# First mixer in three single-pass matmuls per product, its input weights laid out by use, and the expert biases handled ahead of the spatial gating

## The reference, cut to what matters

```
proj = x @ w_in + b_in                      # 1024 -> 512 q, 128 k, 128 v, 512 u, 512 g
attn = sliding_window_attention(q, k, v, sinks)      # 8 query heads, 2 kv heads, window 128
u = gelu(u);  g = layer_norm per group (gelu(g))     # 8 groups of 64
mixed = einsum('gts,bcsgd->bctgd', tril(w_spatial), g) + b_spatial
mix = concat([attn, u * mixed]) @ w_out + b_out
h = layer_norm(alpha * x + mix)
ffn = routed_experts(h, ...)                # 32 experts, top 4, each 1024 -> 2 x 1024 -> 1024
```

## Time and profile before

| what | value |
|---|---|
| median of 3 runs | 1468.22 us (1468.15 to 1469.3) |
| the profiled execution, its own time | 1469.2 us |
| its span | 1467.4 us |
| TensorE busy | 1396.6 us, 95% |
| VectorE, ScalarE, GpSimd busy | 535.3, 341.7, 90.1 us |
| bytes read from HBM | 489.54 MB, 334 GB/s over the span |
| first expert matmul on ring weights | 112.70 us |

### The profile page before, as it was taken

How to read it: one execution, slowest core, us unless ns; L and a number is a source line. 1 busy time by engine, 2 the same in 40 slices (tenths; PEclk the granted TensorE clock), 3 DMA queues, 4 the chain that set the end, 5 groups by cost and what they waited for, 6 DMA issues and landing times.

```text
span 1467.4 us, 23484 instructions
## 1 busy us (share of the span) xinstructions
PE 1396.6 (95%) x10106; PEld 787.6 (54%) x10106; DVE 535.3 (36%) x980; ACT 341.7 (23%) x504; POOL 90.1 (6%) x44
## 2 busy tenths in 40 slices
PE   7999999999999999999998998999999999999998
PEld 6553333333333333333333333333979999899997
DVE  1772111211211111121111111213989658777766
ACT  0531001100100010010000000102765543444442
POOL 0000000000000000000000000002000050122232
PEclk9999999999999999999999999999999999999999
DMA  9699999999999999999999999999544214255552
GB/s 362 261 403 416 428 429 427 428 433 431 430 426 436 430 430 426 435 430 431 429 427 434 427 431 434 430 427 384 182 146 142 77 42 160 91 197 186 191 181 86
DMA packets 37060, 491.36 MB, mean 335 GB/s; under 512 B 4112, under 2 KB 4624, under 8 KB 12592
## 3 DMA queue, kind: packets, MB, share of 16 engines
q1 hardware_dynamic: 36864, 490.47, 80.9%
q10 hardware_dynamic: 144, 0.13, 0.0%
HBM read 489.54 MB, written 1.05 MB: 334 GB/s over the span
## 4 chain that ended last, share of the span: by engine, by line
PE 72%; DMA 24%; DVE 2%; ACT 1%; issue 1%; SPq 0%; DVEq 0%; ACTq 0%
PE bank L905 20%; DMA ring<-in_w_exp 15%; PE bank L934 10%; DMA work<-in_w_exp 8%; PE bank L962 8%; PE bank L963 8%; PE bank L964 8%; PE bank L856 3%; PE bank L844 2%; PE bank L715 2%; PE bank L767 2%; PE bank L685 1%; ACT spare L1551 1%; PE bank L864 1%; PE bank L925 1%; PE bank L920 1%
## 5 line engine op out<-in xcount | busy, mean ns | idle before, releaser
L905 PE MATMUL bank<-ring,spare 128*64 128x512 f32 x1344 | 303.4, 604 | 20.5 <-DMA ring<-in_w_exp 20.3
L2080 DVE TENSOR_SCALAR work<-bank 128x512 f32<-128x512 f32 x32 | 22.1, 692 | 736.6 <-PE bank L905 736.6
L905 PEld LDWEIGHTS bank<-ring,spare 128*64 128x64 f32 x1344 | 97.5, 139 | 214.0 <-issue 183.1
L934 PE MATMUL bank<-ring,spare 128*64 128x512 f32 x672 | 148.8, 595 | 14.7 <-ACT spare L1551 14.7
L963 PE MATMUL bank<-work_parts,ring_parts 128*128 128x256 f32 x568 | 159.3, 281 | 0.0
L1547 ACT ACTIVATE work<-work 128x512 f32<-128x512 f32 x32 | 20.2, 631 | 530.8 <-DVE work L2080 530.8
L905 PE MATMUL bank<-work,spare 128*64 128x512 f32 x576 | 129.6, 600 | 5.3 <-DMA work<-in_w_exp 5.3
L963 PEld LDWEIGHTS bank<-work_parts,ring_parts 128*128 128x128 f32 x568 | 107.7, 190 | 1.1
L934 PEld LDWEIGHTS bank<-ring,spare 128*64 128x64 f32 x672 | 46.9, 137 | 103.1 <-issue 87.4
L962 PE MATMUL bank<-hn_hi,ring_parts 128*128 128x256 f32 x352 | 99.3, 282 | 0.0
L964 PE MATMUL bank<-hn_hi,ring_parts 128*128 128x256 f32 x352 | 99.0, 281 | 0.0
(11 more groups left out here) (467 smaller groups left out, 1980.6 us busy)
## 6 DMA issues: line engine op xcount, KB each, us to landing
ring<-in_w_exp SPq DMA_DIRECT2D x42, 4096.0 KB, 31.6
ring<-in_w_exp SPq DMA_DIRECT2D x42, 2048.0 KB, 26.2
work<-in_w_exp SPq DMA_DIRECT2D x14, 4096.0 KB, 33.0
work<-in_w_exp SPq DMA_DIRECT2D x26, 2048.0 KB, 28.7
spare<-in_w_exp SPq DMA_DIRECT2D x12, 2048.0 KB, 27.8
ring<-in_ffn_up SPq DMA_DIRECT2D x22, 1024.0 KB, 4.8
ring<-in_ffn_down SPq DMA_DIRECT2D x22, 512.0 KB, 3.4
ring<-in_w_in SPq DMA_DIRECT2D x2, 2048.0 KB, 17.2
```

What stands on the lines that cost most here:

```text
L905: ins = pe.matmul(to[n2 * CAP:(n2 + 1) * CAP, :], x_e[:, 4 * j + 2 * half + kk, :], w[:, b, kk, n2 * BANK:(n2 + 1) * BANK], start=False, s ...
L934: ins = pe.matmul(y_bank[n2 * CAP:(n2 + 1) * CAP, :], hidT[:, k % 4, k // 4 * CAP:(k // 4 + 1) * CAP], w[:, kk, n2 * BANK:(n2 + 1) * BANK] ...
```

## The change

- q/k (k = 1 to 7), g and u are computed in three fp32r passes. v, and q/k for k = 0, stay in float32. ScalarE casts x, the q/k columns, g and u to their upper parts (`in_hi`); VectorE subtracts these to get the rests (`in_lo`), in place of the raw weights. TensorE waits for these counts for each k of q/k, and for each half of g and u.
- The input weights are three tensors (w_qkv, w_g, w_u), each contiguous in its columns. The first loads come in five pieces (k = 0, 1, 2 to 3, 4 to 5, 6 to 7). w_g comes ahead of the constants, w_u behind the rows.
- v goes to bank 6; its part for k = 4 to 7 comes behind all of q/k. The scores of tile 0 no longer wait for v.
- u of tile 0 comes ahead of the transposes of the probabilities, u of tile 1 in two halves among and behind them, ahead of the attention matmuls. The spatial mixing stands between the two token tiles of the first half of `project_out`, which starts on each pair of k as its attention copy is ready.
- On SyncE, half of area 0 is issued at proj_done 2, half of area 4 and the other half of area 0 at proj_done 4, x at proj_done 6, and at attn_done 2 the expert biases, the layer norm rows and area 1.
- On VectorE, the first bias subtraction comes ahead of the gating, the second behind it, ahead of the copies of the turned u; the scaling of x comes behind these copies. The mask of wsT goes to GpSimd. Several semaphores are merged and their counts adapted.

```diff
-        w_in = ring[:, 0:KD * 1792].rearrange("p (k n) -> p k n", k=KD)
+        by_k = lambda a, at, n: a[:, at:at + KD * n].rearrange("p (k n) -> p k n", k=KD)
+        w_qkv, w_g, w_u = by_k(ring, 0, W_QKV), by_k(ring, G_AT, G1), by_k(ring, U_AT, G1)
...
-        first_pieces = [slice(0, 1), slice(1, 2), slice(2, 4), slice(4, KD)]
+        first_pieces = [slice(0, 1), slice(1, 2), slice(2, 4), slice(4, 6), slice(6, KD)]
...
@@ sync
-            first_half(APART, 0)
-            sp.wait_ge(attn_done, 1)
-            sp.dma_start(bias_all[0:BIAS_ROWS, :], A["bias"]).then_inc(bias_in, 16)
-            sp.wait_ge(proj_done, 6)
-            for half in range(2):
-                first_half(0, half)
+            sp.wait_ge(proj_done, 2)
+            first_half(0, 0)
+            sp.wait_ge(proj_done, 4)
+            first_half(APART, 0)
+            first_half(0, 1)
+            sp.wait_ge(proj_done, 6)
+            sp.dma_start(x_nat, A["x"].rearrange("(t p) d -> p t d", p=P)).then_inc(ln_rows_in, 16)
+            sp.wait_ge(attn_done, 2)
+            sp.dma_start(bias_all[0:BIAS_ROWS, :], A["bias"]).then_inc(bias_in, 16)
+            sp.dma_start(rows_sb[:, 0:ln2_at], A["rows"][0:ln2_at].partition_broadcast(P)).then_inc(ln_rows_in, 16)
             for half in range(2):
                 first_half(1, half)
-            sp.wait_ge(mixed_done, 1)
+            sp.wait_ge(sgu_done, 1)
             sp.wait_ge(ug_biased, 4)
             first_half(3, 0)
-            sp.wait_ge(mix_first, 1)
+            sp.wait_ge(mix_done, 1)
             first_half(2, 0)
-            sp.wait_ge(mix_done, 4)
+            sp.wait_ge(mix_done, 5)
             first_half(2, 1)
@@ tensor
+            pe.wait_ge(w_in_in[0], 32)
+            for i in range(5):
+                pe.matmul(qk_tile(i), w_qkv[:, 0, qk_cols[i]], xT[:, 0, :], start=i % 2 == 0, stop=False, skip_group_check=True)
+            project_v(0)
+            for piece in range(1, len(first_pieces)):
+                for k in range(first_pieces[piece].start, first_pieces[piece].stop):
+                    pe.wait_ge(in_hi, 2 * piece)
+                    for i in range(5):
+                        pe.matmul(qk_tile(i), qk_hi[:, k, qk_cols[i]], x_hi[:, k, :], start=False, stop=False, skip_group_check=True)
+                    pe.wait_ge(in_lo, 2 * piece - 1)
+                    for i in range(5):
+                        pe.matmul(qk_tile(i), qk_hi[:, k, qk_cols[i]], x_lo[:, k, :], start=False, stop=False, skip_group_check=True)
+                    pe.wait_ge(in_lo, 2 * piece)
+                    for i in range(5):
+                        ins = pe.matmul(qk_tile(i), qk_lo[:, k, qk_cols[i]], x_hi[:, k, :], start=False, stop=k == KD - 1, skip_group_check=True)
+                    if k < KD // 2:
+                        project_v(k)
+            ins.then_inc(proj_done, 1)
+            for k in range(KD // 2, KD):
+                ins = project_v(k)
             ins.then_inc(proj_done, 1)
...
+            def project_half(t, to, hi, lo, before, half):
+                pe.wait_ge(in_lo, IN_PARTS + before + half + 1)
+                for k in range(k_half[half].start, k_half[half].stop):
+                    ins = three_passes(bank[to][:, :], [a[:, k, t * P:(t + 1) * P] for a in (x_hi, x_lo)], (hi[:, k, :], lo[:, k, :]),
+                                       k == 0, k == KD - 1)
+                if half == 1:
                     ins.then_inc(proj_done, 1)
...
+            for half in range(2):
+                project_g(0, half)
+            pe.wait_ge(kv_ready, 3)
+            for half in range(2):
+                project_g(1, half)
+            pe.wait_ge(neg_max, 1)
+            for half in range(2):
+                project_u(0, half)
...
-            ins.then_inc(attn_done, 1)
-            project_half(1, 1, W_QKV)
...
@@ scalar
+            for i, ks in enumerate(first_pieces):
+                if i > 0:
+                    act.wait_ge(w_in_in[i], 32)
+                    act.copy(x_hi[:, ks, :], xT[:, ks, :]).then_inc(in_hi, 1)
+                    act.copy(qk_hi[:, ks, :], w_qkv[:, ks, 0:W_QK]).then_inc(in_hi, 1)
...
@@ vector
+            for half, ks in enumerate(k_half):
+                dve.wait_ge(in_hi, IN_PARTS + 2 + half + 1)
+                less(u_lo[:, ks, :], w_u[:, ks, :], u_hi[:, ks, :]).then_inc(in_lo, 1)
+
             for t, pr in enumerate((prob1, prob0)):
...
+            less_bias(1)
+            dve.wait_ge(sgu_done, 1)
             dve.wait_ge(ug_gelu, 3)
             for b in range(2):
...
             dve.tensor_tensor(u_nat, u_nat, sq, ALU.mult).then_inc(sgu_ready, 1)
-            for n in range(1, SPLITS):
-                dve.wait_ge(bias_cast, n)
...
+            less_bias(2)
             for b in range(2):
-                dve.wait_ge(sguT_done, b + 1)
+                dve.wait_ge(sgu_done, b + 2)
                 dve.tensor_copy(mixT[:, 4 + 2 * b:6 + 2 * b, :], bank[(2, 7)[b]][:, :].rearrange("p (k t) -> p k t", k=2)).then_inc(sguT_ready, 1)
```

More of the change, by code:

```diff
@@ L677, in _, with three_passes @@
         def _(pe):
[L679 to L688, removed]
-                for t in range(TT):
-                    ins = pe.matmul(bank[2][:, T + t * P:T + (t + 1) * P], xT[:, k, t * P:(t + 1) * P], w_in[:, k, W_QK:W_QKV],
-                                    start=False, stop=last, skip_group_check=True)
+            def three_passes(to, left, right, start, stop):
+                pe.matmul(to, left[0], right[0], start=start, stop=False, skip_group_check=True)
+                pe.matmul(to, left[0], right[1], start=False, stop=False, skip_group_check=True)
+                return pe.matmul(to, left[1], right[0], start=False, stop=stop, skip_group_check=True)
@@ new lines, in _, with project_v @@
+            qk_tile = lambda i: bank[i // 2][:, (i % 2) * T:(i % 2 + 1) * T]
+            qk_cols = [slice(i * P, (i + 1) * P) for i in range(5)]
+            def project_v(k):
+                for t in range(TT):
+                    ins = pe.matmul(bank[6][:, t * P:(t + 1) * P], xT[:, k, t * P:(t + 1) * P], w_qkv[:, k, W_QK:W_QKV],
+                                    start=k == 0 and t == 0, stop=k == KD - 1, skip_group_check=True)
+                return ins
+            pe.wait_ge(w_in_in[0], 32)
@@ L731, in _ @@
                 if j == 0:
[L732 to L733 removed]
+                    project_u(1, 0)
                     pe.wait_ge(prob_ready, 2)
@@ L739, in _ @@
                 ins.then_inc(pT_done, 1)
-            project_half(0, 0, W_QKV, range(4, KD))
+            project_u(1, 1)
             pe.wait_ge(pT_ready, 3)
@@ L750, in _ @@
                                         start=pair % 2 == 0 and j == 0, stop=j != 1, skip_group_check=True)
-            ins.then_inc(attn_done, 1)
-            project_half(1, 1, W_QKV)
-            pe.wait_ge(wsT_masked, 1)
-            pe.wait_ge(g_normed, 1)
-            for g in range(NG):
-                ins = pe.matmul(bank[(2, 7)[g // 4]][:, (g % 4) * P:(g % 4 + 1) * P].rearrange("p (c d) -> p c d", c=TT),
-                                wsT[:, g, :], g_nat[:, :, g * GD:(g + 1) * GD],
-                                start=g % 4 == 0, stop=True, skip_group_check=True)
-            ins.then_inc(mixed_done, 1)
+                if pair % 2:
+                    ins.then_inc(attn_done, 1)
             mix_bank = [[0, 1], [5, 6]]
@@ L771, in project_out @@
                 return ins
-            pe.wait_ge(attn_ready, 2)
             pe.wait_ge(w_out_in, 4 * 16)
-            pe.wait_ge(ug_biased, 4)
             project_out(0, range(0, 4))
-            project_out(1, range(0, 4)).then_inc(mix_first, 1)
+            pe.wait_ge(wsT_masked, 1)
             pe.wait_ge(sgu_ready, 1)
+            for g in range(NG):
+                ins = pe.matmul(bank[(2, 7)[g // 4]][:, (g % 4) * P:(g % 4 + 1) * P].rearrange("p (c d) -> p c d", c=TT),
+                                wsT[:, g, :], g_nat[:, :, g * GD:(g + 1) * GD],
+                                start=g % 4 == 0, stop=True, skip_group_check=True)
+            ins.then_inc(sgu_done, 1)
+            project_out(1, range(0, 4)).then_inc(mix_done, 1)
+            pe.wait_ge(sgu_ready, 2)
             for c in range(4):
@@ L1476, in _ @@
                                bias=colv("b_in_qk")[:, i:i + 1]).then_inc(q_ready, 1)
+            act.wait_ge(w_u_wsT_in, 32)
+            for ks in k_half:
+                act.copy(u_hi[:, ks, :], w_u[:, ks, :]).then_inc(in_hi, 1)
             for t, pr in enumerate((prob1, prob0)):
@@ L2652, in _ @@
         def _(pool):
+            pool.wait_ge(consts_in, 32)
+            pool.wait_ge(w_u_wsT_in, 32)
+            pool.tensor_tensor(wsT, wsT, const("upto").unsqueeze(1).broadcast_to([P, NG, P]), ALU.mult).then_inc(wsT_masked, 1)
             pool.wait_ge(split_ready, 1)
```

159 lines of the change are left out of this document (93 added, 66 removed).

## The result

The changed kernel takes 1477.43 us (median of 4 runs, 1476.73 to 1480.55) against 1468.76 us of the kernel before on the same chip; the ratio is 1.0062, 95% interval 1.0049 to 1.0074. The forecast was 1465.9 us. The profiled execution took 1476.73 us with a span of 1474.9 (1467.4 before).

A forecast was written before the change was run, and what follows sets the result against it. Expert weight streaming bounds the kernel, so time moves with the output projection's end: 4.6 us gained there less 2.3 for the lower clock, 1468.2 - 2.3 = 1465.9 us; range 1461.9 to 1469.2.

The forecast's parts named there:

- M: End of the mixer's output projection, 97.63 us before; forecast 95.3 us, with the whole time moving by as much.
- q/k: Split-paced q/k matmul stage: TensorE waits some 1.5 us in two pieces; scores end 3.0 us earlier.
- rival 5: q/k stage runs at the lower clock because of its gaps: slower, about 1478 us; chance 0.07.
- Rival 4: Loads decide: DMA queue over 5 us behind at the output projection's end swallows the gain, about 1468 us; chance 0.11.
- Passes 0.118 and 0.231 us apart: Spacing of three-pass matmuls with 256 and 512 columns in q/k, gate and u; at most 8.5 us gained.
- the arrival of u and probabilities together: Ahead of attention, TensorE's u of tile 0 and VectorE's first probabilities are ready within half a us of each other.
- attention's end: End of the mixer's attention matmuls, forecast at 58.4 us against 59.83 before.
- The bias chain: Expert bias load, cast, subtractions and gating after attention, 20.6 us, delay the output projection's last part to 79.0 us.
- two waits ahead of the last part of the output projection: TensorE stands still 0.7 us ahead of its u transposes and about 3.2 us behind them.
- the half clock: After the second TensorE wait, the last 32 output projection matmuls run at 1.2 GHz, costing 2.3 us.
- rival 2: Bias steps delay the output projection but the clock stays up: gain 4.6 us, 1463.6 us; chance 0.2.
- Rival 3: Bias steps hide after all, for instance through a sooner load: gain 8.2 us, 1460.0 us; chance 0.08.

The follow-up runs named there:

- run 3: Changed kernel with 120 padding instructions ahead of the first expert loop, putting the loop body at its former place within a block: 1468.60 us, ratio 1.0000.
- run 1: Kernel before with only 136 do-nothing wait instructions added on TensorE's queue ahead of the first expert loop: 1476.59 us, ratio 1.0055.
- run 12: run 9 without its 120 padding instructions, so the loop body lies where the change itself puts it: 1473.41 us, ratio 1.0024 to the kernel before.
- run 9: run 8 with VectorE's scaling of the residual rows moved between the two bias subtractions: 1464.79 us, ratio 0.9970 to the kernel before.
- run 7: Kernel before with 392 do-nothing wait instructions added ahead of the first expert loop: 1492.01 us, ratio 1.0156.
- N = 88: Kernel before with 88 do-nothing wait instructions added ahead of the first expert loop: 1471.83 us, ratio 1.0009.
- runs 9 and 10: run 9, and the same with one filling matmul in TensorE's wait ahead of the first layer norm's transposes: 1464.79 and 1464.36 us.
- run 8: run 3 with both expert bias subtractions moved on VectorE behind the gating and the copies the output projection waits for: 1468.4 us, ratio 0.9993.

## Why the prediction was wrong

**The step that failed** is in its first paragraph: "What is issued after M keeps its distance to M in both kernels. So the time moves by as much as M moves." The first expert matmul did keep its distance (15.07 and 15.06 us). What lies behind it did not: the experts' stretch grew by 7.4 us. I had counted everything that the change moves on the queues and engines, and not the instructions themselves. The sum of the profiled executions is: M -1.75, experts +7.4, behind them +1.9, together +7.5, the difference of the spans. The three gaps are 6.5 of the 7.4. What the sum put at nothing, without a term for it, is the place of the loop's code: it costs about 8 us.

By medians the place of the code costs 8.8 us (after against run 3), 8.4 (run 1 against its before) and 8.6 (run 12 against run 9), by the ratios 7.9 to 9.1, more than the 5 to 7 us that the experts show. Behind them, the badly placed kernels' profiled executions take 459.2 to 463.7 us and the well placed ones 456.5 to 461.3. A part of it shows as an issue gap of TensorE among the 64-wide matmuls of the second block; in run 1:

```profile
1188.16 0.41 PE L1208 MATMUL bank<-ring 64*64 64x128 f32 x2 [1.82 <-issue]
```

Run 12 has 1.94 us there and run 7 3.75, the changed kernel 0.64. But N = 88, clean in the loop, has one of 0.91 near it, so where the rest of these 1 to 3 us goes stays open. No kernel was run with a body just short of 8 blocks or just beyond 7 to test the recounted rule, since I found it only behind the runs. That code fetches cause the gaps rests on this: the sequencer stands at the branch itself, fetches run in that time, and the two come and go together in all fourteen kernels.

**What was right.** q/k: TensorE waited twice (0.38 and 0.78 us, forecast some 1.5 in all), and the clock stayed up, so rival 5 was out. Rival 4 was out as well: the DMA queue was idle ahead of M (share 0.03 from 88 to 92 us). Passes 0.118 and 0.231 us apart, the arrival of u and probabilities together, attention's end 0.4 us off. The bias chain as the new limit, with two waits ahead of the last part of the output projection, both put down to VectorE, and the half clock behind the second. But the clock was at the half already for the transposes behind the first wait, which took 1.74 us for 1.04. Sizes were off: the waits were 2.71 and 2.19 us where I had 0.7 and 3.2, their sum 4.9 against 3.9, as the load took 8.6 us for 7.0; the clock cost 1.56 us on the projection and some 0.7 on the transposes, 2.3 as taken. Gain at M: 1.75, forecast 2.3. The argument against rival 2, that each wait over 2.2 us lowered the clock, held here but is no rule: single idle stretches of 2.44 us (run 9) and 2.71 us (at 384.83 in the changed kernel) left it at 1.0, while one of 1.85 us (at 526.28) was followed by 0.72 as the mean of 526 to 532 us.

**Had the loop stayed where it was**, run 3 says 1.0000 (0.9988 to 1.0013), 1466.4 to 1470.1 us. The 1465.9 of the forecast lies just outside; runs 9 and 10, whose first expert matmul is 4.7 and 5.5 us earlier than before, gain 4.5 to 5.0 us, so there the time follows the start of the experts once the code is in place. Run 3 doesn't show it: its profiled execution started them 3.3 us earlier and took 1465.79 us, but the median of ten, 1468.60, has no gain. So no run confirms the forecast's 2.3 us, not even with the loop in place. Rival 3 was mis-sized: hiding the bias chain is worth 5.0 us at M (run 9) or 5.8 (run 8), where I had 5.9 (95.3 less 89.4), but VectorE's queue behind it gives back, all of it in run 8 and 3.6 of 5.0 us in run 9 (M at 89.4 against 94.3 in run 3, first expert matmul at 108.02 against 109.39).

## What to carry to other kernels

When an edit changes how many instructions stand ahead of a long loop, the loop's time can change by itself; here by 7 to 9 us, about twice what run 9, the better order of the same edit, gained. Read the row of instruction fetches and look for issue gaps behind the back edge before looking for a cause in the edit, and compare versions with the loop padded to the same place. A wait on an engine off the path is worth removing only together with what stands behind it in that engine's queue: run 8 made M 5.8 us earlier than run 3 and won nothing clear of the noise until one step was moved into VectorE's own idle time.

## What the runs showed of the hardware that I had not expected

A loop of 1666 TensorE instructions (6.5 blocks of 256) runs without any code fetch after its first iteration where it touches seven blocks (starts at 0.84, 0.99 and 0.18 by the recount, border at 0.76), and with nine in each further iteration where it touches eight (0.37 and 0.62). At a taken back edge the sequencer then stands for 6.1 to 7.1 us in place of 0.3, and 1.9 to 2.8 us of this show as idle time of TensorE. A float32 transpose is one matmul and one weight-load record, a float32 matmul two and two. A wait instruction whose semaphores have been reached costs TensorE's queue about 0.11 us, and up to eight hide behind one full-precision 512-column matmul of 0.87 us. The length of one idle stretch alone doesn't say what the clock does: 2.44 us (run 9) and 2.71 us (changed kernel, 384.83) left it at 1.0, while it was at the half behind another of 2.71 us (changed kernel, 76.39), and behind 4.69 us it was at the half for some 12 us.
